# Second block of a two-block model: norm scales by token, spread by one product, own banks for a layer's first units, gates' rows first, units 4 and 5 loaded ahead

## The chip, the cores and the metric

One core of one Trainium2 chip. The metric is the device time of one execution in microseconds (us), lower is better. The kernel before has a median of 946.09 us over three runs (945.18 to 947.96).

## The reference, cut to what matters

A first block (a modulated mixer and a mixture of 32 experts) gives `x` for 256 tokens of 1024 channels. A second block of two layers follows, and the change lies almost wholly in it.

```python
def rmsnorm_2(x, w):
    y = x * lax.rsqrt(jnp.mean(x * x, axis=-1, keepdims=True) + 1e-6)
    return y * w

def hybrid_layer(x, ...):
    h = rmsnorm_2(x, norm_w)
    proj = h @ w_in                       # 1024 -> 4360 columns
    aq, ak, av, ag, bq, bk, bv, bg, cq, ck, cv, co, cg, ci, cf = split(proj)
    ya = moba_attention(aq, ak, av) * silu(ag)
    yb = head_norm(retention(rotate(bq), rotate(bk), bv)) * silu(bg)
    cq, ck = silu(causal_dwconv([cq, ck]))            # four taps
    yc = mlstm(cq, ck, cv, ci + bias, cf + bias)      # log_sigmoid, cumsum, running maximum
    yc = head_norm(yc * sigmoid(co)) * silu(cg)
    return x + concat(ya, yb, yc) @ w_out

x = rmsnorm(first_block_sum, final_g)     # the first block's last norm
for layer in range(2):
    x = hybrid_layer(x, ...)
return rmsnorm_2(x, final_norm_w)
```

A norm's scale is one number for each token. Since `h @ w_in` is linear in it, the kernel multiplies the unscaled `x` by the weights first and applies the scale when a product is taken out of PSUM.

## The kernel before, in words

All engines run orders written out by hand; semaphores tie them together. The first block streams its weights through a ring of slots in SBUF. Its last step adds the experts' results to `xT` (channels on partitions, tokens along the row) and starts the second block.

In the second block a layer's weights come as 22 units of 1 MB (256 columns, or 128 for unit 2, whose columns are the gates' rows `ci` and `cf`). Units 0 and 1 are the convolution's input `cq`, `ck`; 3 is retention's values, 4 the mLSTM's values, 5 `co`, 6 and 7 the rotated operands, 8 to 17 attention and the other gates, 18 to 21 the output projection. SP loads each unit into `raw[U % 4]`. ACT rounds it to a high half (`high`, line L1293), DVE (for four pieces a layer POOL) subtracts it from the raw value for the low half (`low`, L1299), in two pieces of four 128-row blocks for most units. The low half takes the place of the raw data, so the next load into this place waits until the unit four before is multiplied. PE then runs `tile(l, u, j)`: 24 products of 128x256 (line L1413; high by high, high by low, low by high over eight blocks) into half j of a bank. `pair` does two units block by block, beside the data that arrive. A unit's bank is `bank[3 + U % 3]` with U counted through both layers, so unit 3 waits in `start` until unit 0 is taken out by `conv_in`.

The norm's scale in the kernel before: `stats` (L1443) multiplies the squares by a 128x128 matrix of 1/1024 on PE, which leaves the mean square of every token in all 128 partitions of a 128x256 bank. ACT takes the root (`scale_root`, L1709), DVE the reciprocal over 128x256 (`scale`, L2101 to L2113) and copies it, so that `rs` holds it twice. `scale_columns` (L1458) and `columns_of` bring it back to tokens on partitions for the units laid out by token. In layer 0 there are two such sums over the same `x`, since the first block's last norm and the layer's first are taken together: `squares` and `squares2` (scaled by `final_g`).

Then the layer's front end: `conv_in` (L2121) scales units 0 and 1 into `cp`; `gate_chain` (L1936 to L1959, with `log1p_dve`, L639 to L661) is a chain of 23 small dependent operations on DVE over four rows, interleaved by `take` with the convolution's taps (L1929) and the low halves; ACT enters it in `gate_start` with an Abs and an Exp. Its result goes to PE (`stabilisers`, L1465 to L1472), then `m_rows`, `m_log`, `m_exp`, `m_weigh` (L1995), `m_out` (L1512, L1517) and `m_norm` make the mLSTM. PE's list places these small products between tiles of units. The kernel's end: the last stats, root, reciprocal, copy, and four multiplications of 128x512 (three on DVE, L2265, one on POOL, L1915), each followed by a store.

## Time and profile before

| | us |
|---|---|
| median of three runs | 946.09 (945.18 to 947.96) |
| profiled execution | 944.65 |
| its span on the core | 943.0 |
| PE busy in the span | 876.9 (93%) |
| DVE busy | 414.0 (44%) |
| ACT busy | 310.7 (33%) |
| POOL busy | 36.6 (4%) |

The span runs from the first to the last instruction; 1.65 us of the execution lie around it. The second block begins at about 592 us and fills the rest, so a third of the time is under the change. PE's busy time is modelled from starts and hides how fast it runs; its clock and its idle gaps have to be read by stretch.

### The profile page before, as it was taken

How to read it: one execution, taken by the hardware profiler on the slowest of the kernel's cores; microseconds unless marked ns; L12 is line 12 of the kernel's file. 1: busy time of each engine (PE TensorE's matmuls, PEld its weight loads, DVE VectorE, ACT ScalarE, POOL GpSimd, SP SyncE). 2: the span in 40 equal slices, each digit the busy share in tenths (PEclk: the TensorE clock that was granted, in tenths of full speed). 3: DMA queues.
4: the chain of work that ended last, by engine and by line, in shares of the span. 5: the costliest groups of instructions: out<-in, count | busy, mean ns of one | idle time of the engine just before them, and what ended most of it. 6: DMA issues, size and time to landing. Idle time of an engine off the chain costs nothing.

```text
span 943.0 us, 12754 instructions
## 1 busy us (share of the span) xinstructions
PE 876.9 (93%) x5332; PEld 580.7 (62%) x5332; DVE 414.0 (44%) x778; ACT 310.7 (33%) x564; POOL 36.6 (4%) x23
## 2 busy tenths in 40 slices
PE   5999999999989999899988989989999998999995
PEld 3668874444434443344433433888889898888984
DVE  3187952111101101011111110697887758788772
ACT  4352142111111111111111110757266455726662
POOL 0001000000000000000000000012110001211000
PEclk9999999999999999999999999999999999999998
DMA  9999989999999999999999998453234336233321
GB/s 375 424 426 427 361 355 424 410 427 427 427 426 428 427 428 425 429 426 429 427 427 429 428 422 373 138 220 122 103 135 143 127 112 223 98 126 135 134 91 45
DMA packets 25547, 291.42 MB, mean 309 GB/s; under 512 B 2832, under 2 KB 3344, under 8 KB 4240
## 3 DMA queue, kind: packets, MB, share of 16 engines
q1 hardware_dynamic: 25488, 290.58, 74.9%
q8 instruction: 43, 0.70, 0.3%
q14 instruction: 16, 0.13, 0.0%
...
## 4 chain that ended last, share of the span: by engine, by line
PE 56%; DMA 22%; DVE 14%; ACT 5%; issue 2%; SPq 1%; DVEq 0%; ACTq 0%
PE bank L985 15%; PE bank L1413 15%; DMA ring<-in_expert_w 10%; DMA more<-in_expert_w 10%; PE bank L1017 7%; PE bank L372 3%; DVE lo L1299 3%; DMA ring<-in_ada_w 3%; PE bank L917 2%; PE bank L957 2%; DVE X L342 2%; PE bank L415 1%; PE bank L1443 1%; ACT hi L1293 1%; PE bank L388 1%
## 5 line engine op out<-in xcount | busy, mean ns | idle before, releaser
L985 PE MATMUL bank<-ring,xg 128*64 128x512 f32 x768 | 235.8, 608 | 16.5 <-DMA ring<-in_expert_w 16.5
L985 PEld LDWEIGHTS bank<-ring,xg 128*64 128x64 f32 x768 | 76.0, 140 | 134.1 <-issue 104.5
L1413 PE MATMUL bank<-HH,hi 128*128 128x256 f32 x424 | 126.3, 298 | 9.1 <-DVE lo L1299 9.1
L985 PE MATMUL bank<-more,xg 128*64 128x512 f32 x256 | 117.0, 609 | 7.8 <-DMA more<-in_expert_w 7.8
L1413 PE MATMUL bank<-HL,hi 128*128 128x256 f32 x424 | 120.5, 284 | 0.0
L1413 PE MATMUL bank<-HH,lo 128*128 128x256 f32 x424 | 120.3, 284 | 0.0
L1017 PE MATMUL bank<-ring,X 128*64 128x512 f32 x384 | 113.3, 595 | 0.7 <-ACT X L1057 0.7
L1104 DVE TENSOR_TENSOR X<-X,bank 128x512 f32<-128x512 f32 x16 | 11.0, 688 | 231.1 <-PE bank L985 231.1
L1299 DVE TENSOR_TENSOR lo<-raw,hi 128x1024 fp32r<-128x1024 f32 (+1 forms) x84 | 92.1, 1128 | 7.6 <-ACT hi L1293 7.4
L1413 PEld LDWEIGHTS bank<-HH,hi 128*128 128x128 f32 x424 | 81.7, 193 | 16.2 <-issue 10.2
L1293 ACT ACTIVATE hi<-raw 128x1024 fp32r<-128x1024 f32 (+1 forms) x92 | 86.2, 983 | 13.0 <-DMA raw<-in_units 13.0
L1413 PEld LDWEIGHTS bank<-HL,hi 128*128 128x128 f32 x424 | 81.8, 193 | 1.1 <-issue 1.0
L1117 DVE SCALAR_TENSOR_TENSOR ygL<-bank,small,ygH 128x512 fp32r<-128x512 f32 x32 | 24.0, 751 | 132.9 <-ACT ygH L1064 132.9
L1413 PEld LDWEIGHTS bank<-HH,lo 128*128 128x128 f32 x424 | 81.8, 193 | 0.0
L1017 PEld LDWEIGHTS bank<-ring,X 128*64 128x64 f32 x384 | 34.5, 137 | 50.0 <-issue 47.6
L985 PEld LDWEIGHTS bank<-more,xg 128*64 128x64 f32 x256 | 35.0, 140 | 48.5 <-issue 37.0
L1064 ACT ACTIVATE ygH<-bank,small 128x512 fp32r<-128x512 f32 x32 | 22.0, 687 | 120.0 <-PE bank L1017 120.0
L1028 ACT ACTIVATE xg<-bank,modc 128x256 f32<-128x256 f32 x32 | 13.5, 472 | 141.1 <-PE bank L917 135.6
L1017 PE MATMUL bank<-more,X 128*64 128x512 f32 x128 | 56.6, 595 | 0.7 <-ACT X L1057 0.7
L1299 POOL TENSOR_TENSOR lo<-raw,hi 128x1024 fp32r<-128x1024 f32 x8 | 22.4, 2803 | 731.1 <-ACT hi L1293 731.1
L1045 ACT ACTIVATE X<-bank 128x512 f32<-128x512 f32 x16 | 9.6, 597 | 107.4 <-PE bank L985 107.4
L1413 PE MATMUL bank<-YH,hi 128*128 128x256 f32 x128 | 37.6, 294 | 2.7 <-DVE lo L1299 2.4
...
## 6 DMA issues: line engine op xcount, KB each, us to landing
...
```

What stands on the lines that cost most here:

```text
L342: dve.scalar_tensor_tensor(a, w[:, k, :], cs[:, k:k + 1], a, ALU.mult, ALU.add).then_inc(s_fma, 1)
L372: t = pe.matmul(ps[:, T * j:T * j + T], w[:, k, 128 * (first + j):128 * (first + j) + 128], rhs[:, k, :], start=k == 0, stop=k == 7)
L917: t = pe.matmul(ps[:, T * k:T * k + T], part(ht[:, i, d:d + 128]), part(Pm[q % 2][:, i, :]), start=j == 0, stop=j == 3)
L957: t = pe.matmul(bank[ACC[a]][:, T * k:T * k + T], part(y[:, d:d + 128]), part(PT[n % 2][:, :]), start=n == 0 and k == 0 and j == 0, stop=n ...
L985: t = pe.matmul(bank[3 + i][64 * x:64 * x + 64, :], xg[q % 2][:, k, o + 64 * x:o + 64 * x + 64], place(at[x])[:, k, :], start=k == 0, stop ...
L1017: t = pe.matmul(bank[5 + a][64 * x:64 * x + 64, :], aT[:, f, 64 * x:64 * x + 64], place(at[x])[:, 4 * a + f, :], start=f == 0, stop=f == 3)
L1028: t = act.activation(xg[q % 2][:, k, :], bank[ps][:, T * x:T * x + T], ACT.Identity, bias=shift[:, k:k + 1])
L1064: act.activation(part(ygH[:, 512 * a:512 * a + 512]), bank[5 + a][:, :], ACT.Copy, scale=weight[n % 2]).then_inc(s_ygh, 1)
L1117: dve.scalar_tensor_tensor(part(ygL[:, h]), bank[5 + a][:, :], weight[n % 2], ygH[:, h], ALU.mult, ALU.subtract).then_inc(s_ygl, 1)
L1293: act.activation(part(hi), src, ACT.Copy).then_inc(s_hi, 1)
L1299: e.tensor_tensor(part(lo), src, hi, ALU.subtract).then_inc(signal, 1)
L1413: t = pe.matmul(ps[:, T * j:T * j + T], part(st), part(mv), start=first and a == 0, stop=last and a == 2, skip_group_check=True)
```

## The change: what it does

- The sums of squares are products with the squares as the stationary operand and one or two columns as the moving one (`sum_squares`), two for each block of 128 channels, so a token's mean lies on its own partition in a 128x2 piece. In layer 0 the two sums share one product: `sums` holds the columns 1/1024 and final_g squared / 1024, made at the kernel's start by two DVE operations. The eight squares scaled by `final_g` on ACT go.
- Root, reciprocal and the products between them work on 128x2. The scale is then spread over the partitions: DVE writes a diagonal matrix (`on_diagonals`), PE multiplies it by a matrix of ones (`spread_pe`), DVE copies it out (`rows_of_scale`). `rstd` of the first block is spread in the same way, later. At the kernel's end the last multiplications read the bank itself, all four on DVE, none on POOL.
- `root_table` issues a Sqrt of one element early, once in front of the second block and once in each layer in front of the residual.
- Units 0 to 4 of layer 0 have banks 3, 4, 5, 0, 1; in layer 1 units 0 to 2 have banks 0 to 2. Unit 3 no longer waits for `conv_in`.
- PE finishes unit 2 (the gates' rows) before the last quarter of units 0 and 1, and runs `tile(l, 6, 0)` in front of `stabilisers`, and the second tiles of units 6, 7 and 8 in front of small products that they stood behind. DVE takes the gates' rows out before `conv_in` and orders its low halves anew.
- Units 4 and 5 are loaded to a place of their own, which is that of `YH` and `YL` (the rounded `y` for the output projection), in layer 0 before the second block begins, in layer 1 once the output projection of layer 0 is done. ACT reads them from there; their halves go to the ring's places as before, when units 0 and 1 are multiplied.

The diff, cut to its core ("..." marks what is left out):

```diff
+        def ahead(U):
+            return U % NU in (4, 5)
         def unit_place(U):
+            if ahead(U):
+                return (early0, early1)[U % NU - 4][:, :]
...
+            dve.memset(sums[:, :, 0], 1 / 1024).then_inc(s_gw, 1)
+            dve.scalar_tensor_tensor(sums[:, :, 1], col("fg", 0, 8), 1 / 1024, col("fg", 0, 8), ALU.mult, ALU.mult).then_inc(s_gw, 1)
...
+            def unit_bank(l, u):
+                if u < 3 and l:
+                    return bank[u]
+                return bank[{0: 3, 1: 4, 2: 5, 3: 0, 4: 1}[u] if u < 5 and not l else 3 + u % 3]
...
                     act.wait_ge(*unit_arrival(U))
+                    if ahead(U):
+                        act.wait_ge(s_unit, finished(U - 4))
                     act.activation(part(hi), src, ACT.Copy).then_inc(s_hi, 1)
...
+            def root_table():
+                act.activation(trow[:, 0:1], E6, ACT.Sqrt)
             def residual_act():
+                root_table()
...
-                for U in range(4, 2 * NU):
-                    sp.wait_ge(s_unit, U - 3)
+                for U in range(6, 2 * NU):
+                    sp.wait_ge(s_unit, NU if ahead(U) else finished(U - 4))
...
-                def stats(at, src, k, signal, value):
-                    pe.wait_ge(signal, value)
-                    return pe.matmul(bank[at][:, 0:T], con("ones"), src[:, k, :], start=k == 0, stop=k == 7)
+                def sum_squares(ps, k, weights):
+                    n = weights.shape[1]
+                    for i in range(2):
+                        t = pe.matmul(ps[:, n * i:n * i + n], squares[:, k, 128 * i:128 * i + 128], weights, start=k == 0 and i == 0,
+                                      stop=k == 7, skip_group_check=True)
+                    return t
+                def spread_pe(value, half):
+                    pe.wait_ge(s_rs, value)
+                    pe.matmul(bank[6][:, T * half:T * half + T], con("one", 0, 128), rt[:, :], start=True, stop=True).then_inc(s_rcT, 1)
...
                     if l:
                         take(both, 4)
                         stats_pair(0, 3)
-                        take(both, 4)
+                        take(both, 2)
...
+                    pe.wait_ge(s_hl, 8 * l + 8)
                     tile(l, 2, 0)
+                    spread_pe(11 if l else 6, 0)
+                    take(both, 2)
                     tile(l, 3, 0)
-                    scale_columns(l)
...
+                    tile(l, 6, 0)
                     stabilisers(l)
-                    tile(l, 6, 0)
+                    tile(l, 6, 1)
                     m_rows(l, 0)
                     m_scores(l, 0)
-                    tile(l, 6, 1)
+                    tile(l, 7, 0)
                     m_rows(l, 1)
-                    tile(l, 7, 0)
+                    tile(l, 7, 1)
                     m_out(l, 0)
                     m_scores(l, 1)
-                    tile(l, 7, 1)
                     tile(l, 8, 0)
+                    tile(l, 8, 1)
                     m_out(l, 1)
-                    tile(l, 8, 1)
...
-                for k in range(8):
-                    act.activation(squares2[:, k, :], xT[:, k, :], ACT.Square, scale=col("fg", k)).then_inc(s_sqx, 1)
...
+                def on_diagonals(scale, value):
+                    dve.wait_ge(s_rs, value)
+                    dve.tensor_tensor(spread, ident.unsqueeze(1).broadcast_to([128, 2, 128]), scale.unsqueeze(2).broadcast_to([128, 2, 128]),
+                                      ALU.mult).then_inc(s_rs, 1)
+                def rows_of_scale(value):
+                    dve.wait_ge(s_rcT, value)
+                    dve.tensor_copy(rs[:, :], bank[6][:, 0:T]).then_inc(s_rs, 1)
...
-                pool.tensor_tensor(flat(yT[:, 6:8, :]), flat(yT[:, 6:8, :]), rs2, ALU.mult).then_inc(s_op, 1)
...
+                dve.wait_ge(s_rcT, 4)
+                for i in range(4):
                     dve.wait_ge(s_fin, 2 * i + 4)
+                    dve.tensor_tensor(yT[:, 2 * i:2 * i + 2, :], yT[:, 2 * i:2 * i + 2, :],
+                                      bank[6][:, 0:T].unsqueeze(1).broadcast_to([128, 2, T]), ALU.mult).then_inc(s_od, 1)
```

How the order moves. DVE at the front of layer 0, in the kernel before, from the products of the two norms to the first step of the gates' logarithm (L1299 is a low half, L2121 `conv_in`, L1936 to L1941 the gates' first four operations, L639 the logarithm's first):

```order
L2109 RECIPROCAL rs<-rt 128x256 [waits s_rt2]
L2111 TENSOR_TENSOR rs<-rs,rstd 128x256 [waits s_rs]
L2113 COPY rs<-rs 128x256 [waits s_rs]
L2121 TENSOR_TENSOR scr<-bank3,rs 128x2x256 [waits s_unit,s_fill,s_rs]
L2121 TENSOR_TENSOR scr<-bank4,rs 128x2x256 [waits s_unit,s_fill,s_rs]
L1299 TENSOR_TENSOR lo3<-raw3,hi3 128x1024 [waits s_hi]
L1936 TENSOR_TENSOR X2<-bank5,rs 4x256 [waits s_unit]
L1937 TENSOR_TENSOR X2<-bank5,rs 4x256
L1940 TENSOR_SCALAR X2<-X2,cols 4x256 [waits s_gate]
L1941 TENSOR_SCALAR X2<-X2,cols 4x256
L1299 TENSOR_TENSOR lo0<-raw0,hi0 128x1024 [waits s_hi]
L639 TENSOR_SCALAR rows<-X1 4x256 [waits s_gabs]
```

and now (L1332 is a low half, L2117 a diagonal, L2122 the copy of the spread scale, L1960 to L1965 the gates, L2161 `conv_in`; the logarithm's first step comes right behind the last row):

```order
L2117 TENSOR_TENSOR rt<-cst,small 128x256 [waits s_rs]
L1332 TENSOR_TENSOR lo3<-raw3,hi3 128x1024 [waits s_hi]
L2122 COPY rs<-bank6 128x256 [waits s_rcT]
L1960 TENSOR_TENSOR X2<-bank5,rs 4x256 [waits s_unit,s_rs]
L1961 TENSOR_TENSOR X2<-bank5,rs 4x256
L2161 TENSOR_TENSOR scr<-bank3,rs 128x2x256 [waits s_unit,s_fill]
L2161 TENSOR_TENSOR scr<-bank4,rs 128x2x256 [waits s_unit,s_fill]
L1964 TENSOR_SCALAR X2<-X2,cols 4x256 [waits s_gate]
L1965 TENSOR_SCALAR X2<-X2,cols 4x256
L1332 TENSOR_TENSOR lo0<-early0,hi0 128x1024 [waits s_hi]
L2117 TENSOR_TENSOR rt<-cst,small 128x256 [waits s_rs]
L1332 TENSOR_TENSOR lo1<-early1,hi1 128x1024 [waits s_hi] x2
```

The gates' rows are taken out ahead of `conv_in`, the reciprocal in front of these rows is on 128x2 in place of 128x256, and all of units 4 and 5 is halved in front of the logarithm, where one of those pieces was.

ACT from the first block's last results to the layer's first units, in the kernel before (L1320 rounds `x`, L1802 and L1804 are the two sets of squares, L1709 is the root, L1722 the gates' Abs):

```order
L1802 ACTIVATE scr<-xT 128x512 x3
L1804 ACTIVATE scr<-xT,cols 128x256 x8
L1293 ACTIVATE hi2<-raw2 128x1024 [waits s_ring2]
L1709 ACT_TABLE_LOAD
L1709 ACTIVATE rt<-bank7,small 128x256 [waits s_st2]
L1293 ACTIVATE hi3<-raw3 128x1024 [waits s_ring3]
L1709 ACTIVATE rt<-rs,small 128x256 [waits s_rs]
L1293 ACTIVATE hi3<-raw3 128x1024 [waits s_ring3]
L1293 ACTIVATE hi0<-raw0 128x1024 [waits s_ring0] x2
L1722 ACTIVATE X2<-X2 4x256 [waits s_gate]
L1724 ACT_TABLE_LOAD
L1724 ACTIVATE X1<-X2 4x256 [waits s_gabs]
```

and now (L1353 rounds `x`, L1832 is the one set of squares, L1743 the root, L1756 the gates' Abs; between the first two rows lie the branches of a path that is only taken when an expert overflows and has loads of its own):

```order
L1832 ACT_TABLE_LOAD
L1832 ACTIVATE scr<-xT 128x512 [waits s_sct]
L1832 ACTIVATE scr<-xT 128x512 x3
L1326 ACTIVATE hi2<-raw2 128x1024 [waits s_ring2]
L1743 ACT_TABLE_LOAD
L1743 ACTIVATE small<-bank7,small 128x2 [waits s_st2]
L1326 ACTIVATE hi3<-raw3 128x1024 [waits s_ring3]
L1743 ACTIVATE small<-small 128x2 [waits s_rs]
L1326 ACTIVATE hi3<-raw3 128x1024 [waits s_ring3]
L1326 ACTIVATE hi0<-early0 128x1024 [waits s_unit,s_ahead0] x2
L1326 ACTIVATE hi1<-early1 128x1024 [waits s_unit,s_ahead1] x2
L1756 ACTIVATE X2<-X2 4x256 [waits s_gate]
```

Eight squares are gone, a table load stands in front of the squares as well as in front of the root, and four pieces of units 4 and 5 stand in front of the Abs, where two of unit 4 stood. A further load stands at the head of the second block, in front of the first rounding of a unit:

```order
L1082 ACTIVATE ygH<-bank5,small 128x512 [waits s_sct,s_pg,s_down]
L1082 ACTIVATE ygH<-bank6,small 128x512 [waits s_down]
L1370 ACT_TABLE_LOAD
L1370 ACTIVATE small<-small 128x1
L1326 ACTIVATE hi0<-raw0 128x512 [waits s_ring0,s_down,s_gw]
L1326 ACTIVATE hi1<-raw1 128x512 [waits s_ring1]
L1356 ACTIVATE yT<-xT,small 128x256 [waits s_add]
```

In the kernel before the row L1293 for `hi0` followed the row of `ygH` directly.

## Rows read from the trace of the kernel before

**Rows 1.** The page, part 1: busy us (share of the span) xinstructions.

```profile
PE 876.9 (93%) x5332; PEld 580.7 (62%) x5332; DVE 414.0 (44%) x778; ACT 310.7 (33%) x564; POOL 36.6 (4%) x23
```

**Rows 2.** Windows: stretch, length; PE, PEld, DVE, ACT, POOL busy; PEclk; DMA share, GB/s.

```profile
622.00:640.00 18.00, 15.60 (x112) 14.87 (x111) 17.65 (x35) 8.94 (x17) 0.00 (x0) 0.91 0.38 133
...
632.00:634.00 2.00, 2.00 (x11) 2.00 (x11) 1.93 (x6) 0.00 (x0) 0.00 (x0) 0.50 0.00 0
...
668.00:725.00 57.00, 57.00 (x462) 50.90 (x464) 43.68 (x87) 33.18 (x65) 2.40 (x1) 1.00 0.34 123
...
776.00:780.00 4.00, 2.11 (x18) 1.90 (x16) 2.45 (x4) 0.00 (x0) 0.00 (x0) 1.00 0.33 102
```

**Rows 3.** Timeline, PE, second block: start, length, line, operation [idle before <- releaser].

```profile
631.61 0.58 PE L1413 MATMUL bank<-HH,hi 128*128 128x256 f32 x1 [2.40 <-DVE lo L1299]
...
637.61 0.38 PE L1465 MATMUL bank<-cst,X 4*128 4x4 f32 x2
...
653.58 0.39 PE L1413 MATMUL bank<-HH,hi 128*128 128x256 f32 x1
...
660.98 0.39 PE L1413 MATMUL bank<-HH,hi 128*128 128x256 f32 x1
...
664.88 0.35 PE L1413 MATMUL bank<-HH,hi 128*128 128x256 f32 x1 [0.76 <-DVE lo L1299]
...
780.21 0.36 PE L1413 MATMUL bank<-HH,hi 128*128 128x256 f32 x1 [2.11 <-DVE lo L1299]
...
831.17 0.36 PE L1413 MATMUL bank<-HH,hi 128*128 128x256 f32 x1 [0.79 <-DVE lo L1299]
```

**Rows 4.** Chain of waits, second block: start us, us, what.

```profile
602.32 3.45 PE bank L1443 x16
...
684.35 3.08 PE bank L1413 x24
...
689.34 5.74 PE bank L1413 x48
...
771.50 0.86 PE bank L1443 x4
```

**Rows 5.** Timeline, PE, the first block: the same columns.

```profile
122.94 1.03 PE L476 MATMUL bank<-cst,scr 128*128 128x1 f32 x8
```

**Rows 6.** Timeline, DVE, layer 0 up to unit 9.

```profile
620.79 1.33 DVE L639 TENSOR_SCALAR rows<-X 4x256 f32<-4x256 f32 x1 [1.08 <-ACT X L1724]
...
635.78 0.41 DVE L1959 TENSOR_TENSOR X<-X 4x256 f32<-4x256 f32 x1
...
654.65 1.02 DVE L1995 SCALAR_TENSOR_TENSOR X<-bank,X 128x384 f32<-128x384 f32 x2
...
663.52 2.35 DVE L1299 TENSOR_TENSOR lo<-raw,hi 128x1024 fp32r<-128x1024 f32 x2
```

**Rows 7.** Timeline, ACT, the front of layers 0 and 1.

```profile
590.59 1.14 ACT L1293 ACTIVATE hi<-raw 128x512 fp32r<-128x512 f32 x2
...
592.29 0.91 ACT L1323 ACTIVATE yT<-xT,small 128x256 f32<-128x256 f32 x2 [0.56 <-DVE xT L1092]
...
606.59 1.28 ACT L1709 ACT_TABLE_LOAD   x1
...
616.19 2.01 ACT L1293 ACTIVATE hi<-raw 128x1024 fp32r<-128x1024 f32 x2 [3.57 <-DMA raw<-in_units]
...
618.61 0.42 ACT L1722 ACTIVATE X<-X 4x256 f32<-4x256 f32 x1 [0.41 <-DVE X L1941]
...
786.63 0.42 ACT L1724 ACTIVATE X<-X 4x256 f32<-4x256 f32 x1
```

**Rows 8.** Timeline, ACT and DVE, the kernel's end.

```profile
932.26 1.28 ACT L1709 ACT_TABLE_LOAD   x1
...
934.06 1.75 DVE L2259 RECIPROCAL rs<-rt 128x256 f32<-128x256 f32 x1 [3.28 <-ACT rt L1709]
...
936.18 2.96 DVE L2265 TENSOR_TENSOR yT<-yT,rs 128x512 f32<-128x512 f32 x3
```

228 lines of the change are left out of this document (113 added, 115 removed).

## The prediction

> **What bounds the kernel now.** I read the page's busy times first, then stretches of the second block (from 592 us on), then PE's idle gaps with what ended them, and last the chain of waits and DVE's and ACT's timelines through the front of layer 0. PE is busy 93% of the span, DVE 44%, ACT 33% [rows 1]. The stretches show that this is an average over two regimes. From 668 to 725 us PE is busy 57.00 of 57.00 us at full clock, so there only PE work counts [rows 2]. From 622 to 640 us DVE is busy 17.65 of 18 us and PE 15.60, with a mean clock of 0.91 [rows 2]: there the chain of the gates' small operations on DVE, between low halves and taps, is the bound. PE's gaps say the same. The first tile of unit 5 waits 2.40 us for a low half, the first of unit 9 waits 0.76 us, and in layer 1 unit 2 waits 2.11 us and unit 9 0.79 us [rows 3]. The third place is the kernel's end, a chain over ACT and DVE with PE empty [rows 8].
>
> The clock: after the gap of 2.40 us it stood at 0.50 (1.2 GHz of 2.4) between 632 and 634 us, while around the gap of 2.11 us it stayed at 1.00 [rows 2]. From 631.61 to 637.61 us PE ran a tile and a half, 36 products [rows 3]. At full clock 48 products take 5.74 us [rows 4], so 36 take 4.3, plus about 0.2 for the first behind a gap: the fall cost 1.5 us.
>
> Prices used below: an isolated tile of 24 products 3.08 us, two in a row 5.74 [rows 4]; a product of 256 fp32 columns 3.45 / 8 = 0.43 us [rows 4]; a product with one column, 1.03 us less an overlap of some 0.07 for four, so 0.24 each [rows 5].
>
> **The start of the second block.** `root_table` puts a table load and a root of one element in front of ACT's two pieces at 590.59 us. A load takes 1.28 us, and I take 0.13 for the root. ACT had 0.56 us of idle time before it writes `yT` at 592.29, and PE's first product follows that at once [rows 7]. So PE starts 1.28 + 0.13 - 0.56 = 0.85 us later. The order shows that it buys nothing in layer 0: the loads of the overflow path in between make a second load in front of the squares and a third in front of the root. Those two are hidden. The squares that go cost ACT some 3.3 us, and PE is 0.9 us behind.
>
> **Layer 0's front.** The stats: 8 + 8 products at 0.43 become 16 at 0.24, 6.90 to 3.84 us. Half of the 6.90 stood behind the pair's seventh block. The first group starts at 602.32 [rows 4] + 0.85 = 603.2 and ends at 607.0. PE then does unit 2, 3.08 us, to 610.1. Meanwhile the scale's chain has two roots on ACT with a 1.0 us piece between, seven operations on 128x2 at about 0.2, one low half of 1.1 and the diagonal of 0.42 on DVE; with the hops I get 610.3. So `spread_pe` waits 0.2 and takes 0.43: 610.8. The last quarter of units 0 and 1 takes 3.08: 613.9. Here the loading ahead counts. ACT waited 3.57 us for unit 4's data before 616.19 [rows 7]; now it starts at 613.9, when units 0 and 1 are done. It has four pieces (2 x 2.01 [rows 7]) in front of the Abs, then 0.42 for the Abs, 1.28 for the Exp's load, 0.42 for the Exp and 0.1 of hops: DVE can start the logarithm at 620.1, against 620.79 [rows 6].
>
> From there to the chain's last operation before, at 635.78 + 0.41 = 636.19, it took 15.40 us [rows 6], with two low halves and eight taps inside. Now two low halves (unit 6's), nine taps and the copy of `rstd` are inside: 15.40 + 0.40 + 0.35 = 16.15, so 636.25. Before, PE reached the stabilisers only at 637.61 because of the slow clock [rows 3]. Now it has done one tile more by then (613.9 + 5.74 + 5.74 + 3.08 + 0.6 + 5.74 = 634.8) and waits some 1.5 us for DVE. It goes on at 636.35.
>
> From the stabilisers to the end of `m_scores(1)` the kernel before had three tiles and the small products, 653.58 - 637.61 = 15.97 us [rows 3]. Now there are three tiles too (6, 7, 7): 652.3. Before, DVE started the second pair of `m_weigh` at 654.65 and gave PE unit 9 at 664.88, 10.23 us later [rows 3, 6]. Now this pair waits for `m_scores(1)`, which the move of `tile(7, 1)` put behind another tile: 652.2 + 10.23 = 662.4. Gain at unit 9: 2.4 us. From 653.58 to 660.98 PE had two tiles and `m_out(1)`, 7.40 us [rows 3]; the same now ends at 659.7, so PE waits 2.7 us in place of 0.76.
>
> **Layer 1's front**, on the clock of before. `stats_pair(0, 3)` starts at 771.50 [rows 4], four products at 0.24 in place of 0.86 us: 772.5. Half of the pair's rest and unit 2 in one run: 5.74, 778.2. Unit 2 no longer waits for its low half, which DVE makes first, so the 2.11 us gap goes. The spread takes 0.43 and the last quarter 3.08: 781.7. ACT's four pieces, Abs, load and Exp as above: 787.9, against 786.63 + 0.42 = 787.05 [rows 7]. So here the chain of the gates starts 0.9 us later than before, since the pair ends later. It ends at 787.9 + 15.8 = 803.7 (no `rstd`). Then 15.97 + 10.13: unit 9 at 829.9, against 831.17 [rows 3], gain 1.3 us. Again PE waits 2.7 us there in place of 0.79.
>
> **Behind the fronts** PE is the bound and nothing is removed. The six other stats pairs take 0.96 in place of 0.86 us: 0.6 us lost. The first block's two new operations on DVE lie beside a wait for PE.
>
> **The end.** Before: load 1.28 at 932.26, root of 256 columns, reciprocal 1.75, copy 0.29, then three multiplications in 2.96 us to 939.14 [rows 8]. Now: root at 932.5 (the table is there), 0.2, reciprocal 0.2, diagonal 0.42, product 0.43 with 0.1 of latency, 933.9; four multiplications with no POOL beside them, some 0.62 apart: 936.4. Gain 2.7 us, bounds 2.0 (as slow as 0.99 each for the first two) and 3.1 (the last store stands alone).
>
> **Sum.** 2.4 + 1.3 - 0.6 + 2.7 = 5.8 us, the start's 0.85 being in the 2.4. Against it stands the clock: PE waits 2.7 us in front of unit 9 in both layers. A gap of 2.40 brought the clock down and one of 2.11 did not, so each has about an even chance, at 1.5 us, which the PE-bound stretch behind does not give back. I take one fall: 5.8 - 1.5 = 4.3. The profiled execution took 944.65 (span 943.0 and 1.65 around it): 940.35. The runs' median is 1.44 above it, so 941.8.
>
> **Two rules of the Trainium skill.** The load in front of the last root starts at 932.26, and the reciprocal behind that root at 934.06, 1.80 us later [rows 8], with a load of 1.28 and so 0.52 for the root and the hops. The skill's page "ScalarE: Activation LUTs", section "What ACT_TABLE_LOAD costs", adds a drain of 1.38 us to each switch. By that the block would start 1.4 us later still, and the sum would be 2.9; the rows have no room for such a drain, and I go by the row.
> A gap of 2.40 us was followed by a clock of 0.50 [rows 2, 3]. The page "TensorE: Matmul & The Clock Gate", section "Why this matters for your kernels", warns only of idle gaps longer than the ones I forecast. By it neither fall comes, which is the first rival.
>
> **Rivals.**
> - No fall of the clock: 5.8 us, 940.3. For it the gap of 2.11 us that left the clock up; against it the one of 2.40. Chance 0.20.
> - Both fall: 2.8 us, 943.3. Same rows. 0.20.
> - The fronts give nothing, only the end does. The chain on DVE is as long as before, and if the gates' chain starts no earlier than before in either layer and the low halves of unit 6 delay the taps, unit 9 comes at its old time: 2.7 - 0.6 = 2.1, 944.0. For it: in layer 1 I find the chain's start late already. Chance 0.17.
> - Slower: ACT takes its four pieces of units 4 and 5 before the Abs, and cannot start them before the last quarter of units 0 and 1, which itself stands behind `spread_pe`. If the scale's chain is late, PE is blocked with that quarter unissued, and everything moves one for one. My chain has 0.2 us of wait in layer 0. The change is slower once the logarithm starts about 2.2 us later than I forecast in both layers (2 x 2.2 = 4.3). At 3.5 us each: 941.8 + 7.0 = 948.8. Against it: nine hops of some 0.1 us, all seen in the trace. Chance 0.05.
> - More: DVE's 10.23 us from `m_weigh` to unit 9 holds operations slowed beside POOL; if they fall apart, unit 9 comes 2 us earlier in each layer and no gap brings the clock down: 937.8. Chance 0.08.
>
> The forecast itself has 0.30. The range that leaves out a tenth on each side is 938.6 to 945.2. A difference of 0.3% (2.8 us) is about what a measurement of this kernel can tell from no change: faster means below 943.25. The forecast, the first and the last rival lie there, and half of the second, and with the spread of about 1 us around each I get 0.69 faster, 0.23 the same, 0.08 slower.
>
> **What would show it.** PE's first product of the block 0.85 us later against the last results of the experts. Three table loads of ACT between 590 and 607. Unit 5 without the gap of 2.40; the stabilisers near 636.4 with a gap in front; unit 9 near 662.4 behind a gap of 2.7. In layer 1 no gap in front of unit 2, and unit 9 at 829.9 less what layer 0 gained. The granted clock behind both gaps. From the end of the last stats to the last multiplication 4.0 us in place of 6.8. It is wrong if the logarithm starts later than 621, if unit 9 waits for something other than its low half, or if the end gains under 2 us.

## The result and the profile after

The changed kernel takes 951.11 us (median of 10 runs, 948.53 to 953.07), the kernel before 946.32 us (10 runs, 944.81 to 947.96). The ratio is 1.0050, with a 95% interval of 1.0037 to 1.0063: 4.8 us slower, where I had forecast 941.8 us and given "slower" 0.08. The profiled execution took 951.28 us with a span of 950.0, against 944.65 and 943.0 before.

The page's first part (engine, busy us and share of the span, instructions) and the clock's line of its second part:

```profile
PE 882.6 (93%) x5368; PEld 584.2 (61%) x5368; DVE 414.0 (44%) x785; ACT 309.5 (33%) x559; POOL 39.3 (4%) x22
...
PEclk9999999999999999999999989998999999899998
```

PE is 5.7 us longer busy than in [rows 1], though its sums and the spread are fewer columns of work than the sums and transposes before. That is the first hint that PE ran part of its work at the lower clock. The windows say where (busy us of each engine in the stretch, then the granted clock):

```profile
622.00:640.00 18.00, 14.34 (x117) 13.91 (x116) 17.69 (x32) 7.74 (x12) 4.58 (x2) 1.00 0.48 176
640.00:648.00 8.00, 8.00 (x35) 6.96 (x36) 2.74 (x6) 7.75 (x10) 0.00 (x0) 0.57 0.00 1
668.00:725.00 57.00, 55.87 (x450) 49.86 (x451) 46.17 (x90) 29.61 (x60) 2.41 (x1) 1.00 0.34 118
760.00:764.00 4.00, 4.00 (x24) 4.00 (x23) 2.59 (x5) 3.50 (x7) 0.00 (x0) 0.57 0.28 115
811.00:819.00 8.00, 7.89 (x33) 6.95 (x34) 2.96 (x6) 7.61 (x11) 0.00 (x0) 0.57 0.00 0
```

In [rows 2] there was one stretch at 0.50, from 632 to 634 us. Now, apart from the kernel's end, where it is down in both kernels, the clock is down in three places of the second block: for nearly 7 us behind 640, again behind 811, and for under 4 us behind 760. PE's starts, with the idle time in front in brackets:

```profile
595.60 0.70 PE L1442 MATMUL bank<-yT,raw 128*128 128x256 f32 x2 [0.95 <-ACT yT L1356]
```
```profile
639.89 0.35 PE L1502 MATMUL bank<-cst,X 4*128 4x4 f32 x2 [3.48 <-DVE X L1983]
```
```profile
669.13 0.35 PE L1449 MATMUL bank<-HH,hi 128*128 128x256 f32 x1 [2.83 <-DVE lo L1332]
```
```profile
758.55 0.69 PE L1481 MATMUL bank<-cst,scr 128*128 128x1 f32 x5 [0.90 <-ACT scr L1916]
```
```profile
811.11 0.35 PE L1502 MATMUL bank<-cst,X 4*128 4x4 f32 x2 [3.68 <-DVE X L1983]
```
```profile
840.42 0.36 PE L1449 MATMUL bank<-HH,hi 128*128 128x256 f32 x1 [2.83 <-DVE lo L1332]
```

The gap of 2.40 us in front of unit 5 and that of 2.11 us in front of unit 2 of layer 1 [rows 3] are gone, as forecast. In their place PE waits 3.48 and 3.68 us in front of the stabilisers (L1502) for the last operation of the gates' chain (L1983). Unit 9 comes at 669.13 against 664.88, and in layer 1 at 840.42 against 831.17.

Why the chain is late stands in DVE's timeline, beside POOL's:

```profile
618.11 2.34 DVE L1332 TENSOR_TENSOR lo<-early,hi 128x1024 fp32r<-128x1024 f32 x2
620.75 2.12 DVE L655 TENSOR_SCALAR rows<-X 4x256 f32<-4x256 f32 x1 [0.30 <-ACT X L1758]
622.90 1.74 DVE L658 RECIPROCAL rows<-rows 4x256 f32<-4x256 f32 x1
```
```profile
629.06 2.34 DVE L1332 TENSOR_TENSOR lo<-raw,hi 128x1024 fp32r<-128x1024 f32 x2
631.33 0.47 DVE L1952 SCALAR_TENSOR_TENSOR scr<-scr,cols 128x256 f32<-128x256 f32 x1
631.72 2.62 DVE L671 SCALAR_TENSOR_TENSOR rows<-rows 4x256 f32<-4x256 f32 x1
```
```profile
639.34 0.40 DVE L1983 TENSOR_TENSOR X<-X 4x256 f32<-4x256 f32 x1
```
```profile
616.86 5.86 POOL L1332 TENSOR_TENSOR lo<-early,hi 128x1024 fp32r<-128x1024 f32 x1 [543.37 <-ACT hi L1326]
630.20 3.86 POOL L1332 TENSOR_TENSOR lo<-raw,hi 128x1024 fp32r<-128x1024 f32 x1 [7.48 <-ACT hi L1326]
```

And POOL's same two operations in the kernel before:

```profile
618.28 3.70 POOL L1299 TENSOR_TENSOR lo<-raw,hi 128x1024 fp32r<-128x1024 f32 x1 [544.59 <-ACT hi L1293]
642.06 2.45 POOL L1299 TENSOR_TENSOR lo<-raw,hi 128x1024 fp32r<-128x1024 f32 x1 [20.08 <-ACT hi L1293]
```

Two of DVE's small operations end 0.15 and 0.28 us behind the end of a POOL operation. L655 (one 4x256 operation) runs from 620.75 to 622.87, POOL's `lo` to 622.72. The second: L671 from 631.72 takes 2.62 us, to 634.34, and POOL's `lo` ends at 634.06. Without POOL beside them they take 0.28 and 0.41 us (below). In the kernel before, the first did the same for a shorter time (1.33 us at 620.79 [rows 6], with POOL's `lo` until 621.98), and the second POOL operation stood behind the chain, at 642.06. The earlier order on ACT brought it forward to 630.20, into the chain. So the chain takes 620.75 to 639.74, 19.0 us, where the forecast had 16.15. In layer 1 POOL's first operation (788.74 for 3.26 us) falls on DVE's three low halves (below, 5.70 us in place of 3.4) instead of on the logarithm, and its second (801.65 for 3.97) again on L671 (3.06 us for two). One more such meeting is in both kernels and in all the runs below: just ahead of the low halves that unit 9 waits for, DVE's L2001 (at 665.27) takes 2.58 us beside POOL's next `lo` (665.03 for 2.53). No run moves that one, so what it costs is not shown.

```profile
788.52 5.70 DVE L1332 TENSOR_TENSOR lo<-early,hi 128x1024 fp32r<-128x1024 f32 x3
```

The end: sums, root, reciprocal, diagonal, product, multiplications:

```profile
940.81 1.47 PE L1481 MATMUL bank<-cst,scr 128*128 128x1 f32 x8 [0.66 <-ACT scr L1916]
942.32 0.26 ACT L1743 ACTIVATE small<-bank,small 128x2 f32<-128x2 f32 x1 [0.76 <-PE bank L1481]
942.62 0.17 DVE L2302 RECIPROCAL small<-small 128x2 f32<-128x2 f32 x1 [2.52 <-ACT small L1743]
942.81 0.42 DVE L2117 TENSOR_TENSOR rt<-cst,small 128x256 f32<-128x256 f32 x1
...
943.29 1.22 PE L1497 MATMUL bank<-rt,cst 128*128 128x256 f32 x2 [1.01 <-DVE rt L2117]
944.55 2.48 DVE L2307 TENSOR_TENSOR yT<-yT,bank 128x512 f32<-128x512 f32 x4 [1.31 <-PE bank L1497]
945.26 2.13 SPq L1416 DMA_DIRECT2D out<-yT  x4
```

From the last sums to the span's end it is 9.2 us, against 11.5 before (931.50 to 943.0).

The balance of the two profiles, at unit 9 of layer 0, at layer 1's `stats_pair(0, 3)`, at unit 9 of layer 1 and at the last sums: after is late by 4.25, 5.83, 9.25 and 9.31 us, and by 7.0 at the end of the span. Of the 4.25, 1.9 us were there before the second block began: the experts' last group of products started at 593.43 against 591.53. In the profiles of the other kernels with this same first block it started anywhere from 590.9 to 594.0, so these 1.9 us are run to run and not the change's.

### The profile page after: what moved, and what is told of

It reads as the page before. It is cut to its first block, busy times and chain, and to the rows that moved or that the text cites. A ratio compares the mean times of both kernels' runs of the same rounds, so it can differ in the third digit from the quotient of the medians.

```text
span 950.0 us, 12843 instructions
## 1 busy us (share of the span) xinstructions
PE 882.6 (93%) x5368; PEld 584.2 (61%) x5368; DVE 414.0 (44%) x785; ACT 309.5 (33%) x559; POOL 39.3 (4%) x22
## 3 DMA queue, kind: packets, MB, share of 16 engines
HBM read 289.52 MB, written 1.05 MB: 306 GB/s over the span
## 4 chain that ended last, share of the span: by engine, by line
PE 60%; DMA 22%; DVE 12%; ACT 3%; issue 2%; SPq 1%; DVEq 0%; ACTq 0%
PE bank L1449 18%; DMA ring<-in_expert_w 17%; PE bank L1003 15%; PE bank L1035 7%; PE bank L388 3%; DMA more<-in_expert_w 3%; DVE lo L1332 3%; DMA ring<-in_ada_w 2%; PE bank L975 2%; PE bank L935 2%; DVE X L358 2%; PE bank L431 1%; PE bank L404 1%; PE bank L1481 1%; DVE rows L671 1%
## 5 line engine op out<-in xcount | busy, mean ns | idle before, releaser
L1003 PE MATMUL bank<-ring,xg 128*64 128x512 f32 x768 | 240.8, 612 | 16.0 <-DMA ring<-in_expert_w 16.0
L1003 PE MATMUL bank<-more,xg 128*64 128x512 f32 x256 | 120.1, 623 | 8.1 <-DMA more<-in_expert_w 8.1
L1332 DVE TENSOR_TENSOR lo<-raw,hi 128x1024 fp32r<-128x1024 f32 (+1 forms) x78 | 84.6, 1120 | 4.3 <-ACT hi L1326 4.2
L1326 ACT ACTIVATE hi<-raw 128x1024 fp32r<-128x1024 f32 (+1 forms) x84 | 78.1, 975 | 0.1
L1449 PE MATMUL bank<-hi,HH 128*128 128x256 f32 x128 | 38.1, 298 | 0.2 <-POOL lo L1332 0.2
```

Source lines behind the costliest of these rows:

```text
L1003: t = pe.matmul(bank[3 + i][64 * x:64 * x + 64, :], xg[q % 2][:, k, o + 64 * x:o + 64 * x + 64], place(at[x])[:, k, :], start=k == 0, stop ...
L1326: act.activation(part(hi), src, ACT.Copy).then_inc(s_hi, 1)
L1332: e.tensor_tensor(part(lo), src, hi, ALU.subtract).then_inc(signal, 1)
L1449: t = pe.matmul(ps[:, T * j:T * j + T], part(st), part(mv), start=first and a == 0, stop=last and a == 2, skip_group_check=True)
```

## The experiments

Each was timed in turn with the kernel before on one chip; "before" is 945.99 to 946.62 in the four groups. Between two kernels of different groups the two intervals together leave about 2 us uncertain.

**1. POOL's two low halves out of the gates' chain.** In the first kernel DVE makes both (edit: the last number pair of `POOLED`), in the second POOL makes unit 7's behind the chain:

```diff
-POOLED = ... if i == 1 and u in (4, 7, 10, 13))
+POOLED = ... if i == 1 and u in (10, 13))          # p1_dve_low
+POOLED = ... if i == 1 and u in (7, 10, 13))       # p2_pool_waits
                 for l in range(2):
+                    pool.wait_ge(s_gate, 23 * l + 23)   # p2_pool_waits
                     pool_low(l, 7)
```

> The kernel after, with the second halves of units 4 and 7 (lo, 128x1024) made by DVE and not by POOL, in both layers; POOL keeps those of units 10 and 13 and the rotations. My theory: in the kernel after these two POOL operations (616.86 for 5.86 us, 630.20 for 3.86 us) lie inside the chain of the gates, and one of DVE's operations waits for the end of each (2.12 us against 1.33, 2.62 against 0.41); that makes PE wait 3.48 us in front of the stabilisers, and the half clock behind that gap costs 3.0 us more. Without them the chain takes 16 us in place of 19.0, PE waits under 1 us there, the clock stays up, and unit 9 comes 5 us earlier in each layer, unless DVE's 2 x 1.2 us of more work delay it: 942 us (941 to 945), 1.0 of ratio against the kernel after below 0.993. Rival (the chain is long because of the order on DVE, two low halves and nine taps in it): the chain stays at 18 us or more and the time at 950 or above. Rival 2 (the gap in front of the stabilisers goes, but the clock falls at the gap in front of unit 9 that takes its place): 945.

> The kernel after, with unit 4's second half made by DVE, and unit 7's second half still by POOL but only once the gates' chain is done. No POOL operation lies inside the chain then, and DVE has one 1.2 us operation more, in front of the chain. My theory (POOL's operations hold DVE's up): same as the run in which DVE makes both, 942 us, within 1 us of it, chain 16 us. If DVE's additional work were what counts, the two runs would differ by 1 us a layer. Rival (order on DVE): 950 or above.

Measured: 942.27 us for the first (ratio to before 0.9948 [0.9930, 0.9966]) and 939.39 for the second (0.9926 [0.9914, 0.9939]), 8.8 and 11.7 us less than after. Taking POOL's two pieces of 1024 columns a layer out of the chain turns the change from slower to faster. DVE in the second kernel:

```profile
619.96 0.28 DVE L655 TENSOR_SCALAR rows<-X 4x256 f32<-4x256 f32 x1
620.27 1.74 DVE L658 RECIPROCAL rows<-rows 4x256 f32<-4x256 f32 x1
```
```profile
629.11 0.40 DVE L671 SCALAR_TENSOR_TENSOR rows<-rows 4x256 f32<-4x256 f32 x1
```
```profile
634.51 0.41 DVE L1984 TENSOR_TENSOR X<-X 4x256 f32<-4x256 f32 x1
```
```profile
635.06 0.35 PE L1502 MATMUL bank<-cst,X 4*128 4x4 f32 x2 [0.64 <-DVE X L1984]
```

The same operations take 0.28 us (L655) and 0.85 us for two (L671, 3.06 for two in after). The chain runs 619.96 to 634.92, 15.0 us in place of 19.0, and PE waits 0.64 us at the stabilisers. The two kernels differ by 2.9 us where I expected 1, with intervals that overlap. Their traces show no reason in the chain (gap 0.65 and 0.64 us, 0.39 in layer 1 of both); the clock of the first was down from 607 to 615 us, of the second from 606 to 610.

**2. Each of the two POOL operations.** Here unit 4's stays on POOL and in the chain, unit 7's waits:

```diff
                 for l in range(2):
+                    pool_low(l, 4)
+                    pool.wait_ge(s_gate, 23 * l + 23)
                     pool_low(l, 7)
```

> The kernel after (951.11 us), in which POOL still makes the second halves of units 4 and 7, but that of unit 7 only once the gates' chain is done. Of the two POOL operations that lie in the chain in after, the first (5.86 us from 616.86) stays there, the second (3.86 us from 630.20) goes out. p2_pool_waits, with both out of it, took 939.39. Theory: each of the two costs by the DVE operation that waits for its end, 2.12 - 0.28 = 1.8 us for the first and 2.62 - 0.41 = 2.2 us for the second, a layer; and PE's gap in front of the stabilisers, 3.48 us with both and 0.65 with none, would be 1.3 to 2. With the second out, 2.2 us a layer come back, and the part of the clock loss that hangs on the gap's length, 1.5 us of the 3: 943.5 to 947. Rival (only the sum of both matters, as PE waits otherwise anyway): 950. Rival 2 (the first costs nothing, as DVE's additional operation in p2 is as long): 940.

Measured: 944.41 us (0.9985 [0.9971, 0.9999]). So unit 7's, the one that the change moved into the chain, cost 951.11 - 944.41 = 6.7 us, and unit 4's 944.41 - 939.39 = 5.0 (6.2 and 5.6 by the ratios, each with some 1.8 to either side). In the trace L655 takes 2.10 us again, L671 0.85 for two, and PE waits 1.26 and 1.45 us at the stabilisers.

**3. The same edit on the kernel before** (unit 4's second half by DVE):

```diff
-POOLED = ... if i == 1 and u in (4, 7, 10, 13))
+POOLED = ... if i == 1 and u in (7, 10, 13))
```

> The kernel before, with the second half of unit 4 (lo, 128x1024) made by DVE and not by POOL in both layers. In before POOL made it from 618.28 for 3.70 us, and the first operation of the gates' logarithm, begun at 620.79, took 1.33 us and ended when POOL did; in p2_pool_waits the same operation took 0.28 us. Theory: that operation is 1.0 us shorter in both layers, the DVE's 1.2 us more lie where DVE waited 1.08 us for the Exp; unit 9 comes up to 1 us earlier and its gap of 0.76 us goes: 945 to 946.6, a gain of 0 to 1.6 us, far less than the 11.7 us that p2_pool_waits gained on the kernel after. Rival (what p2_pool_waits gained is a gain that any kernel gets by keeping POOL off): 940.

Measured: 942.33 us (0.9958 [0.9944, 0.9971]), 4.2 us faster, more than I expected. The operation is 1.05 us shorter, the gap of 2.40 us in front of unit 5 becomes 1.35, and behind it the clock no longer falls. At unit 9 only 1.06 us of that arrive in layer 0 (counted from the experts' last group) and 1.07 in layer 1 (counted from the sums before it): the clock's part is lost there in waiting for DVE. The two profiled runs differ by 2.3 us; where the other 1.9 of the medians' 4.2 come from stays open. So POOL in the chain was a cost of the kernel before too, and the change itself, with POOL out of the chain on both sides, is worth 2.9 us (939.39 against 942.33; 3.0 by the ratios, with 1.7 to either side) and not the 7.2 by which p2_pool_waits is faster than before.

**4. The gap and the clock.** First a real tile of PE put ahead of the stabilisers, then useless products in the gap:

```diff
+                    tile(l, 6, 1)
                     stabilisers(l)
-                    tile(l, 6, 1)
+                    tile(l, 7, 0)
                     m_rows(l, 0)
                     m_scores(l, 0)
-                    tile(l, 7, 0)
-                    m_rows(l, 1)
                     tile(l, 7, 1)
+                    m_rows(l, 1)
```

> The kernel after, with PE one tile further on in both layers: tile (6, 1) stands in front of the stabilisers, tile (7, 0) between them and m_rows(0), tile (7, 1) between m_scores(0) and m_rows(1). DVE and POOL are as in the kernel after, so the chain stays at 19.0 us. My theory: the gap of 3.48 us in front of the stabilisers shrinks to 0.4 us and the clock stays up there, which gives back 3.0 us in each layer; the tile is not lost, but PE has one less behind, so the gap in front of unit 9 (2.83 us) grows or stays as DVE ends m_weigh: between 943 and 946 us. Rival (what is lost is the chain's length alone, and the clock at these places costs nothing as PE waits for DVE in any case): unit 9 comes where it came and the time stays within 1.5 us of 951. Rival 2: the clock falls at the larger gap in front of unit 9 instead, 948.

```diff
                 def stabilisers(l):
                     pe.wait_ge(s_late, 16)
+                    for k in range(26):
+                        pe.matmul(bank[2][:, 0:T], part(HH[:, k % 8, 0:128]), part(HH[:, k % 8, :]), start=True, stop=True)
                     pe.wait_ge(s_gate, 23 * l + 23)
```

> The kernel after with 26 products (HH against itself, 128x256, into bank 2, not used by anything) issued by PE in front of its wait for the gates, in both layers: they take 26 x 0.12 = 3.1 us of the idle time of 3.48 and 3.68 us there. DVE, ACT and POOL are unchanged. Theory: behind the gap the clock stood at 0.50 for 7 us, in which PE did what takes 4 us less 0.5; without the idle time it stays up, or falls for one stretch of 4 us only, and 1.5 to 3 us come back in each layer: 945 to 948. Rival (the clock falls for the small products around the stabilisers, whatever stands in front): 950 to 951.

Measured: the real tile gives 950.41 us (1.0043 [1.0027, 1.0059]), no difference from after that can be told; the useless products give 946.10 (0.9998 [0.9984, 1.0012]), 5.0 us faster than after, with a chain of 19.0 us as in after (621.40 to 640.40). Nothing that the kernel needs was taken away or moved in the second, so these 5.0 us are clock. The profiles show where: from the stabilisers to unit 9 after takes 29.24 us in layer 0 and 29.31 in layer 1, the kernel with the useless products 27.73 and 26.26, together 4.6 less. Its windows and those of the real tile:

```profile
632.00:640.00 8.00, 8.00 (x69) 7.97 (x67) 7.86 (x16) 0.07 (x1) 2.71 (x1) 1.00 0.39 140
640.00:648.00 8.00, 7.72 (x42) 6.61 (x42) 3.65 (x9) 7.51 (x11) 0.00 (x0) 0.79 0.05 11
810.00:820.00 10.00, 9.93 (x70) 8.69 (x71) 6.27 (x14) 9.60 (x15) 2.23 (x2) 1.00 0.30 107
```
```profile
632.00:640.00 8.00, 7.36 (x57) 6.72 (x55) 7.86 (x19) 1.70 (x5) 0.60 (x1) 1.00 0.49 167
640.00:648.00 8.00, 6.66 (x28) 6.07 (x28) 1.27 (x3) 6.90 (x7) 0.00 (x0) 0.57 0.23 96
814.00:818.00 4.00, 4.00 (x21) 3.78 (x21) 0.00 (x0) 3.95 (x5) 0.00 (x0) 0.57 0.00 0
```

With the products in the gap, the clock is down for under 4 us in place of nearly 7 behind 640 and not at all behind 810. With the tile ahead it is down for nearly 7 us in layer 0 although PE waited only 0.60 us: PE then waited 1.38 us more for unit 7's low half, right behind the stabilisers' products of four rows. So my theory, that a smaller gap would keep the clock up, was wrong for the tile: two short waits and the small products between them were as bad as one long wait in layer 0, and in layer 1 (0.80 and 1.38 us) the clock was still down for under 4 us. And PE, a tile further on, now waits 4.11 us for unit 9's low half in both layers in place of 2.83, with a fall behind that wait too (667 and 838 us), where after had none. In layer 0 unit 9 comes 73.65 us behind the block's first product, in after 73.53. So both rivals of the expectation have their part: PE waits for DVE in any case, and the fall comes at the larger gap.

**5. Sums with one column.** The weights of a product repeated over 128 columns (64 for each of layer 0's two sums):

```diff
-                    n = weights.shape[1]
+                    n = 128
-                        t = sum_squares(bank[6], k, con("ones", 0, 1))
+                        t = sum_squares(bank[6], k, con("ones"))
-                            t = sum_squares(bank[7], k, sums[:, k, :])
+                            t = sum_squares(bank[7], k, sums[:, k, :].unsqueeze(2).broadcast_to([128, 2, 64]))
```

> The kernel p2_pool_waits (939.39 us) with the sums of squares as wide products: the weights of a product (scratch against ones) are repeated over 128 columns in place of 1 (over 64 each in place of one for the two sums of layer 0), and the means are read at a stride of 128 or 64. Number of products the same. In the trace of the kernel after the clock fell between 760 and 764 us, right behind a gap of 0.90 us and eight records with one column; in p1_dve_low, p2_pool_waits, p3_tile_ahead and p4_no_first_load it fell at the 16 sums of layer 0 (604 to 607 us), in p1, p3 and p4 behind that same gap at 757 to 761 too; in the kernel before, whose sums have 256 columns, at neither place. Theory A (products with one column let the clock fall): the clock stays up at 606 and at 757 us; 1.5 to 3 us back, less what 128 columns cost more than one (0 to 0.19 us a product, by 0.43 for 256 columns and 0.24 for one: 0 to 1.5 us on the sums behind the fronts): 937 to 939.4 us. Rival (the gaps in front of them do it): the falls stay and the time is 939.4 to 941.

> The kernel after with the sums of squares as wide products (weights repeated over 128 columns) and nothing else; POOL's operations stay in the gates' chain. In q1_wide_sums the same edit took 3.4 us off p2_pool_waits, and the clock fell at one place in place of four. Theory: the clock no longer falls at the sums (760 us in after's trace; 604 to 607 in four others), while the falls at the stabilisers, behind gaps of 3.48 and 3.68 us, stay: 951.1 - 3.4 = 947.7, and 946.5 to 949. If the whole of the loss against before came from the products with one column, 946. Rival (behind the gaps the clock is down anyway): 950.5.

Measured: 935.99 us on top of p2_pool_waits (0.9892 [0.9875, 0.9909]), 3.4 us less, and 949.15 on top of after (1.0035 [1.0023, 1.0046]), 2.0 us less. I had expected 0 to 2.4 us of the first and 3.4 of the second. The second interval overlaps that of after, so these 2.0 us alone would not be clear of noise. A record of the wide product is 0.27 us long, one with few columns 0.25, so the columns cost nearly nothing. The stretch of layer 0's sums, in p2_pool_waits and in q1_wide_sums:

```profile
604.00:612.00 8.00, 8.00 (x55) 7.95 (x55) 5.68 (x13) 4.16 (x6) 0.00 (x0) 0.79 0.48 177
```
```profile
604.00:612.00 8.00, 7.60 (x64) 7.34 (x63) 5.59 (x13) 4.72 (x7) 0.00 (x0) 1.00 0.65 236
```

It falls during or behind the narrow sums in seven of the eight profiles that have them in layer 0 (after is the eighth), and in none of the five with wide ones; at 756 to 764 us, behind a gap of 0.90 us, in six of eight and in none of five. The clock costs the kernel after about as much here as my whole allowance for it.

**6. The end alone, on the kernel before** (two layer-1 products with 256 columns become four with one, table load ahead, root and reciprocal on 128x2, diagonal, one product, four multiplications on DVE):

```diff
-                        t = stats(6, squares, k, s_sqy, 4 * l + i + 1)         # kept for layer 0
+                            for h in range(2):
+                                t = pe.matmul(bank[6][:, h:h + 1], squares[:, k, 128 * h:128 * h + 128], con("ones", 0, 1), ...)
...
                     high(l, 21)
+                    if l:
+                        act.activation(trow[:, 0:1], E6, ACT.Sqrt)
...
-                scale_root(bank[6][:, 0:T], s_st2, 4)
+                act.activation(small[:, 314:316], bank[6][:, 0:2], ACT.Sqrt, bias=E6).then_inc(s_rt2, 1)
...
+                pe.matmul(bank[6][:, 0:T], con("one", 0, 128), rt[:, :], start=True, stop=True).then_inc(s_rcT, 1)
```

> The kernel before, with the end of the kernel after and nothing else of the change: layer 1's four last sums of squares by token (four products with one column in place of two with 256), the table load for the last root ahead of layer 1's last squares, the root on 128x2, the scale spread by one product, four multiplications on DVE and none on POOL. From the last sums (931.50 in before, 940.81 in after) to the span's end it took 11.5 us in before and 9.2 us in after. My theory: 2.3 us less, 0.3 us of it lost to the products with one column, so 2.0 us faster than before, 944.6. Rival: the end gains nothing by itself (the stores set it): 946.6. Rival 2: the clock falls in front of the end because of the one-column products: 946.

Measured: 943.82 us (0.9970 [0.9958, 0.9982]), 2.7 us faster. From the last sums (933.71) to the span's end (942.9) it is 9.2 us, as in after.

**7. Without the table load at the start of the residual**, on after and on q1_wide_sums:

```diff
             def residual_act():
-                root_table()
```

> The kernel after without the one-element root and its table load at the start of the residual (residual_act); the two later ones (in front of each layer's last squares) stay. My theory, from the prediction: PE starts the second block 0.85 us earlier, so 0.85 us off the time: 950.3. The first block is not touched: its last product of the experts lay 1.9 us later in the profile of after than in that of before (591.79 against 589.88), and if that is from run to run it lies within 589 to 592.5 here. Rival: the load at the start spares a load later on; then the time is the same or longer.

> The kernel q1_wide_sums (935.99 us) without the one-element root and its table load at the start of the residual. PE's first product of the second block follows ACT's yT, for which it waits 0.95 us in q1; in p4_no_first_load there was no such wait. Theory: 0.85 us less, 935.1, since with the falls of the clock at the sums gone nothing else moves in between. Rival: the load is needed later in front of the first scale's root and would cost there; in the trace of the kernel after there is a load behind the squares at 607.04 in any case, so I give it 0.1.

Measured: 950.71 (1.0042 [1.0028, 1.0056]) against 951.11, and 937.40 (0.9905 [0.9890, 0.9919]) against 935.99: no gain that can be measured. In the traces the load in front of the squares (602.59 in after) is gone too, so that one load is left (603.54 and 605.31) as in before: the load ahead had added two. The 0.95 us wait for `yT` is gone in both, and from the experts' last group to the stabilisers PE takes 42.4 us in place of 43.3 (r4 and q1), 0.9 less. It is lost again in r4's profile, where the clock is down at 638, 802 and 829 us, in q1's at 637 alone. Why it fell more often there stays open.

**8. Without the loading ahead** (units 4 and 5 through the ring again, on p2_pool_waits):

```diff
         def ahead(U):
-            return U % NU in (4, 5)
+            return False
-                for U in range(6, 2 * NU):
+                for U in range(4, 2 * NU):
```

> The kernel p2_pool_waits without the loading ahead: units 4 and 5 come through the ring of four buffers again, as in the kernel before, each asked for when the unit four places in front of it is done. Theory: ACT, which in the kernel before waited 3.57 us for unit 4's data in front of 616.19, waits about as long again in layer 0 and somewhat less in layer 1, and the Abs and the Exp stand behind these pieces: the gates' chain starts 3 us later in each layer, PE waits at the stabilisers and the clock falls for longer: 944 to 948 us against 939.4. Rival (hidden, since the chain has waited for something else): 939.4 to 940.5.

Measured: 956.96 us (1.0110 [1.0093, 1.0127]), 17.6 us more, far over my 5 to 9. In the new order ACT makes the pieces of unit 4 and of unit 5 ahead of the Abs, where before only unit 4's stood there, so it waits for both loads, one behind the other:

```profile
618.12 2.00 ACT L1326 ACTIVATE hi<-raw 128x1024 fp32r<-128x1024 f32 x2 [9.57 <-DMA raw<-in_units]
622.16 2.01 ACT L1326 ACTIVATE hi<-raw 128x1024 fp32r<-128x1024 f32 x2 [2.03 <-DMA raw<-in_units]
...
625.78 0.42 ACT L1758 ACTIVATE X<-X 4x256 f32<-4x256 f32 x1
```

The logarithm starts at 626.23, where p2_pool_waits has it at 619.96: 6.3 us later, not 3. Of the change's parts this is the one that carries the others: without it the new order is slower than the kernel before by 10.5 us.

**9. `m_scores(1)` ahead of its tile again**, on q1_wide_sums, and then useless products in the two gaps that are left:

```diff
-                    tile(l, 7, 1)
                     m_out(l, 0)
                     m_scores(l, 1)
+                    tile(l, 7, 1)
                     tile(l, 8, 0)
                     tile(l, 8, 1)
                     m_out(l, 1)
+                    filler(8)        # s2_fill_both; and filler(4) in front of the wait for the gates
                     tile(l, 9, 0)
```

> The kernel q1_wide_sums (935.99 us) with one part of the change's order on PE undone: tile (7, 1) stands behind m_out(0) and m_scores(1) again, as in the kernel before, in both layers. In q1 DVE waits 1.14 us for m_rows(1) and 1.69 us for m_scores(1), whose products stand behind that tile, and PE then waits 2.82 us in front of unit 9 for the low half that DVE makes behind them. Theory: m_scores(1) ends 3.0 us earlier, DVE's second pair of m_weigh starts 1.69 us earlier and unit 9 with it, the gap in front of it shrinks to 1.1 us: 2 x 1.7 = 3.4 us less, 932.6. Rival (the tile was put there to cover a wait of PE for m_weigh(0) in front of m_out(0), and the gap comes up there in its place): 935 to 937.

> The kernel r2_scores_first (934.92 us) with such products in its two remaining gaps of a front: 4 in front of the wait for the gates (gap 0.62 and 0.38 us) and 8 in front of unit 9 (gap 1.28 us). In r2's trace the clock fell behind the stabilisers in both layers, for 4 us each, 1.5 us lost each. Theory A (it falls for the gaps): these falls go, 3 us less, 932. Theory B (it falls for the products of four rows and the short waits between them, which stay): 934.5 to 935.5.

Measured: 934.92 us (0.9879 [0.9865, 0.9894]) and 931.31 (0.9848 [0.9832, 0.9864]). In the first, unit 9's gap is 1.28 us in place of 2.82 in both layers. It comes 25.98 us behind the stabilisers in place of 27.72 in layer 0, with one fall of the clock between the two marks in either kernel: the mechanism and its 1.7 us are as expected. In layer 1 it is 25.99 in place of 26.23 only, since the clock fell there (802 us) and in q1_wide_sums it did not. The time gained only 1.1 us, within what the runs spread (932.3 to 936.7 and 935.1 to 939.5). In the second no stretch of the second block before the very end is below full clock (below, first the first kernel's windows, then the second's):

```profile
636.00:642.00 6.00, 5.38 (x30) 4.82 (x29) 4.12 (x10) 4.82 (x8) 4.80 (x1) 0.74 0.30 127
802.00:808.00 6.00, 6.00 (x33) 5.45 (x34) 3.17 (x4) 5.94 (x7) 1.75 (x1) 0.72 0.08 15
```
```profile
632.00:640.00 8.00, 7.93 (x61) 7.20 (x60) 6.18 (x14) 4.69 (x8) 4.67 (x1) 1.00 0.34 132
640.00:648.00 8.00, 7.80 (x60) 6.16 (x62) 5.88 (x13) 7.96 (x13) 2.71 (x3) 1.00 0.37 131
800.00:810.00 10.00, 9.93 (x79) 8.13 (x77) 7.66 (x15) 9.94 (x16) 2.62 (x3) 1.00 0.29 107
```

That kernel is 14.7 us faster than before and 19.8 us faster than after. The products in the gaps go to a bank that is written again before anyone reads it. They take away the short waits and leave the stabilisers' products of four rows; the falls are gone in the profile, and the four runs lie within 930.9 to 933.4, so it was the waits (theory A), as far as one kernel shows it.

## Why the prediction was wrong, step by step

- **What bounds the kernel**: right. The chain on DVE through the front of each layer sets the time, and PE behind it.
- **The start, +0.85 us and three table loads**: right in size (0.95 us of waiting, gone without the load; from the experts' last group to the block's first product 2.17 us against 1.33) and in number (ACT loads at 592.61, 602.59, 607.04).
- **Layer 0 up to the logarithm**: better than forecast. The sums took 3.5 us (3.84), PE waited 0.29 us for the spread (0.2), and from the block's first product to the logarithm it was 25.15 us, where I had 26.4.
- **The gates' chain, 16.15 us: this step failed.** I took the 15.40 us of before and added a tap and a copy. I counted what DVE issues there and not what POOL does beside it. I had found that DVE's 1.33 us operation at 620.79 [rows 6] was in the chain and did not ask why a 4x256 operation took so long, so the 15.40 already held 1.05 us of waiting for POOL, and that the new order would move a second POOL operation in was not priced at all. The chain took 19.0 us with POOL's two operations in it and 15.0 without them. Layer 1: 16.8 against 15.8 forecast, and DVE came 1.6 us late to its start (794.14, with the Exp done at 792.59), since three low halves took 5.70 us beside POOL's.
- **PE's wait at the stabilisers, 1.5 us**: 3.48 and 3.68, as a result.
- **15.97 us from the stabilisers to `m_scores(1)`**: 18.95, since the clock was down for 7 us. **10.23 us from there to unit 9, and the gap of 2.7 us**: right, 10.19 and 2.83.
- **The clock, one fall of 1.5 us behind unit 9's gap: this step failed too**, in place and in size. It stayed up behind 2.83 us in both layers of this profile, and fell for nearly 7 us at each set of stabilisers and for under 4 us at layer 1's sums. By the stretches that is 3.0 + 3.0 + 1.5 us in place of 1.5, an estimate, and so 6.0 of the 9.3 us between forecast and result. Shown: 5.0 us for the falls at the stabilisers (s1_fill_gap), and 3.4 us for those at the sums once POOL is out of the chain (q1_wide_sums; 2.0 in r3_wide_alone, not clear of noise). That the falls at the stabilisers were so long follows from the step before (with POOL out of the chain they lasted under 4 us or did not come); those at the sums do not follow from it: in the prediction the sums had their duration as their only price.
- **The six other pairs of sums, -0.6 us**: right as a duration, see above for what it left out.
- **The end, 2.7 us gained**: right. 2.7 us by the runs (q2_tail_only), 2.3 by the profiles.
- **The rivals and the signs**: the slower rival had the right region and the wrong cause. It wanted a logarithm some 3.5 us late in each layer; counted from the block's first product it was 1.25 us early in layer 0, and counted from the sums 0.4 us late in layer 1. Of "no fall of the clock" it is true that none came behind unit 9's gap, and three came elsewhere. None of the three things that I had said would show the prediction wrong happened (logarithm later than 621, unit 9 waiting for something else, the end under 2 us): all lie outside the stretch that failed, from the logarithm to the stabilisers. I had put the rule of the Trainium skill beside it (page "TensorE: Matmul & The Clock Gate", section "Why this matters for your kernels"), which warns only of gaps longer than the forecast ones. Behind the 3.48 and 3.68 us at the stabilisers the traces agree with it; they do not where the clock fell behind much shorter waits beside small products, as at 637 us in q1_wide_sums, behind 0.64 us.

With POOL out of the chain the same kernel takes 939.39 us, inside the range that I gave, and chain, wait and gap are each within 1.2 us of the forecast. That is in part luck: the forecast's chain still held one wait for POOL, as r1_one_waits has it (944.41 us, in the range as well, 2.6 above the forecast), and p2_pool_waits has four falls of the clock in its profile where I had one. What the two show is that the neighbour left out turned the sign.

That neighbour is told of in the Trainium skill, page "SBUF — State Buffer", section "Who interferes with whom": a DVE instruction with two inputs from SBUF, or in one of the modes that use both ports, and a GpSimd instruction that reads SBUF exclude each other, and the loser is blocked for the other's whole length. This case's traces agree: a DVE operation that was held ended behind POOL's by about its own length (0.15, 0.28 and 1.08 us for L655, L671 and a low half, which take 0.28, 0.41 and 1.21 alone). L655 has one input, so by that rule it would have to run in such a mode, which no row here shows. The POOL operation alone takes 2.41 us (at 695.15 in after); counted back from its end at 622.72 it began in earnest at 620.31, about when DVE's low halves ended (620.45) and DVE stood idle for 0.30 us, so it had been held for some 3.5 of its 5.86 us; then DVE's L655 was held until it ended. The second time: 634.06 - 2.41 = 631.65, just ahead of L671 (631.72), which was held, though DVE had no pause there. In layer 1 788.74 + 3.26 - 2.41 = 789.59 lies between two low halves that DVE ran without a pause; the second of them was held and took 3.43 us. So POOL was kept out by one unbroken row of DVE operations for 3.5 us and let into two others, and what decides the turn is open. In each case one operation of DVE, however small, paid 1.8 to 2.3 us.
